# NSA's compressed branch in a slot table: minimum, exponential, normalising, transposes and evictions in slots of their own, probabilities transposed six slots behind

## The chip, the core and the metric

One core of a Trainium2 chip runs the whole program in one launch. The metric is the device time of that core in microseconds, the median of several runs. The engines are TensorE (PE, with its weight loads as PEld), VectorE (DVE), ScalarE (ACT), GpSimd (POOL) and SyncE (SP), which issues the DMAs. Each engine takes its instructions in the order in which the program wrote them, and the engines meet through semaphores.

## What is computed

One decoder layer over 512 tokens of width 1024: an input projection, three token mixers (NSA, a differential attention, a forgetting attention), gated merging, and a feed-forward part with a causal convolution. The change is in the compressed branch of the first mixer, NSA: each query looks at 31 compressed key blocks.

```python
def nsa_attention(q, k_cmp, v_cmp, k_slc, v_slc, k_win, v_win, gate_logits, cmp_end):
    ...
        dist_c = tpos[:, None] - cmp_end[None, :]
        s_c = jnp.einsum('btgrd,bngd->bgrtn', qg, k_cmp).astype(jnp.float32)
        s_c = s_c - sl[..., None] * dist_c.astype(jnp.float32)
        p_c = masked_softmax(s_c, dist_c >= 0)
        o_c = jnp.einsum('bgrtn,bngd->btgrd', p_c.astype(v_cmp.dtype), v_cmp)
        ...
        o = gc[:, :, 0] * o_c + gc[:, :, 1] * o_s + gc[:, :, 2] * o_w
```

With 512 tokens and eight selected blocks of 64 the selection takes every block, so the selected branch is plain causal attention (`slc`), beside a window of 256 (`win`).

## The kernel before, in words

Matrices are split into a high and a low part, and a product takes three matmuls (two where one factor is exact enough). While the attention of NSA runs, TensorE also works through the merge gates: 192 matmuls of 512 columns (G, "gate matmuls"), 40 of them before the attention's first unit, 152 spread over its slots. Weights for them arrive by DMA and are split by ScalarE (W, `wh`) and VectorE (WL, `wl`) in pieces of 512 columns.

`attention_events` (L121) writes the order of the stage as a table of slots, and every engine walks through the same list of events and does its own part of each. One slot is one *unit* j of 64: a query block i of 128 rows, one of eight heads, `slc` or `win`. A unit is

- S.j: TensorE two score matmuls over the unit's keys (128 to 512 columns) into bank 6 or 7; VectorE adds the bias and takes the minimum (`prob_n`, `nmx`, L1232); ScalarE takes the exponential and its sum (L867).
- C.j, for every second unit: VectorE forms the reciprocal and the coefficient (L1247, L1249), and GpSimd scales the two units' probabilities (L1470).
- Four units make a group, and each key block of a group is a step n: TA.n four transposes of `prob_n` on TensorE (L1559) into bank 4 or 5; EH.n ScalarE's high part `ptn_h` (L917); EL.n VectorE's low part `ptn_l` (L1267), which frees the bank for TA.n+2; VA.n two matmuls with the values (L1793, L1795) into bank 2 or 3, by the half g of the heads.
- When both groups of one g are through, OX.i.g copies half of the bank on ScalarE (`otmp_n`, L922), and VectorE sums it with the other half (`osum_n`, L1282, two instructions) and so frees the bank; OY.i splits the result for the projection.

The compressed branch adds for each query block i one job:

- SC.i: TensorE writes the scores of all eight heads with one matmul of 256 columns and sixteen of 32 columns (L1764 to L1768) into bank 2; VectorE takes minimum, difference and slope (L1303, L1304, L1307); ScalarE takes the exponential (L905).
- CN.i: VectorE sums, inverts, weighs by the gate and multiplies (L1312 to L1319).
- TC.i: TensorE transposes (L1774) into bank 2; ScalarE copies the high part `pcT` (L911); VectorE forms the low part (L1272).
- OC.i.g: TensorE multiplies with the compressed values (L1780), as the first product into bank 2 + g of block i.

Query block i begins at slot 16 i. SC.i stands in slot 16 i + 3, CN.i in + 5, TC.i in + 7. The first transposes of a group come `t_lag` = 5 slots behind its last unit, its first product three slots after them. Within a slot the tuple `order` (L220) sorts the events. For SC and TC all engines' parts stand in the same slot, since an event has one place in the list. The bank holds one result after the other in the order of the list: the sums of block i - 1, SC.i, TC.i, then block i; `begin` on TensorE waits until the result before has been taken.

## Time and profile before

| | us |
|---|---|
| median of three runs | 978.65 |
| the runs | 976.17, 978.65, 978.80 |
| the profiled execution | 978.79 |
| its span on the core | 977.0 |
| TensorE busy in it | 958.5 |
| VectorE busy | 559.8 |
| ScalarE busy | 426.2 |
| mean granted clock of TensorE | 0.996 |

The page says that TensorE is at work for nearly the whole span; "busy" counts a matmul from its start to a modelled end, so that rows overlap. The NSA stage lies at about 103 to 213 us: block 0 until 116, block 1 (units 16 to 31) until 138, block 2 until 168, block 3 until 200, then the last transposes and products without units. Everything before and behind it is projections, the other mixers and the feed-forward part.

### The profile page before, as it was taken

Reading aid. Unit: us, or ns where it says so; the run is one execution under the profiler, and the core shown is the slowest. Engines: PE = TensorE matmul, PEld = TensorE weight load, DVE = VectorE, ACT = ScalarE, POOL = GpSimd, SP = SyncE. Lnnn points to the kernel's source line nnn. Section 1 sums busy time; section 2 is a strip of 40 time slices with the busy share of each in tenths; the row PEclk is TensorE's granted clock in tenths of the full one; section 3 lists DMA queues with packets and bytes.
Section 4 is the critical chain, followed back from the end, with each engine's and each line's share of the span. In section 5 each row is a group of like instructions: output and inputs, shape, how many; then the busy total and the mean of one; then the engine's idle time right before and its main releaser. Section 6 shows DMA issues by size and latency. Waiting matters only on the chain.

```text
span 977.0 us, 12185 instructions
## 1 busy us (share of the span) xinstructions
PE 958.5 (98%) x4625; PEld 794.5 (81%) x4625; DVE 559.8 (57%) x1063; ACT 426.2 (44%) x770; POOL 209.8 (21%) x250
## 2 busy tenths in 40 slices
PE   6999999999999999999999999999999999999998
PEld 5787877788888888888888888888888888888887
DVE  6737787864366895546567454655655665522113
ACT  5335776754256653445777333423222322221110
POOL 3000457640001112212455220121112121100000
PEclk9999999999999999999999999999999999999999
DMA  6512110112222212222211242223222322232222
GB/s 237 219 44 86 45 44 1 43 45 86 87 89 85 87 44 87 86 87 87 81 50 44 87 172 87 87 89 123 91 87 87 121 95 86 87 117 99 87 87 86
DMA packets 13691, 86.33 MB, mean 88 GB/s; under 512 B 1473, under 2 KB 1985, under 8 KB 4289
## 3 DMA queue, kind: packets, MB, share of 16 engines
q1 hardware_dynamic: 13632, 85.55, 24.2%
q8 instruction: 37, 0.61, 0.3%
q14 instruction: 22, 0.17, 0.1%
HBM read 83.44 MB, written 2.10 MB: 88 GB/s over the span
## 4 chain that ended last, share of the span: by engine, by line
PE 89%; DVE 7%; ACT 2%; issue 2%; DMA 0%; SPq 0%; ACTq 0%; DVEq 0%
PE ps L1531 22%; PE ps L1533 22%; PE ps L1532 22%; PE ps L1715 10%; PE ps L1559 4%; PE ps L1672 1%; PE ps L1671 1%; PE ps L1700 1%; DVE prob_n L1232 1%; DVE wl L1013 1%; PE ps L1586 1%; DVE ptn_l L1267 1%; PE ps L1793 1%; PE ps L1795 1%; DVE prob L1232 1%
## 5 line engine op out<-in xcount | busy, mean ns | idle before, releaser
L1013 DVE TENSOR_TENSOR wl<-raw,wh 128x512 fp32r<-128x512 f32 (+2 forms) x118 | 173.5, 1475 | 136.4 <-ACT wh L701 133.8
L701 ACT ACTIVATE wh<-raw 128x2048 fp32r<-128x2048 f32 (+1 forms) x58 | 109.4, 1886 | 157.9 <-PE ps L1533 140.3
L1531 PE MATMUL ps<-aT_h,wh 128*128 128x512 f32 (+1 forms) x376 | 146.7, 390 | 0.8 <-DVE aT_l L1022 0.8
L1532 PE MATMUL ps<-aT_l,wh 128*128 128x512 f32 (+1 forms) x376 | 146.4, 389 | 0.0
L1533 PE MATMUL ps<-aT_h,wl 128*128 128x512 f32 (+1 forms) x376 | 146.4, 389 | 0.0
L1531 PE MATMUL ps<-wh,aT_h 128*128 128x512 f32 x256 | 102.0, 398 | 0.0
L1533 PE MATMUL ps<-wh,aT_l 128*128 128x512 f32 x256 | 100.0, 391 | 0.0
L1532 PE MATMUL ps<-wl,aT_h 128*128 128x512 f32 x256 | 99.8, 390 | 0.0
L1514 POOL TENSOR_TENSOR gl<-gl,rstdT 128x512 f32<-128x512 f32 x22 | 44.5, 2022 | 234.5 <-ACT gl L987 234.5
L1470 POOL TENSOR_SCALAR prob_n<-prob_n,coef 128x384 f32<-128x384 f32 (+3 forms) x64 | 67.7, 1071 | 114.6 <-DVE coef L1249 114.3
L1531 PEld LDWEIGHTS ps<-aT_h,wh 128*128 128x128 f32 (+1 forms) x376 | 70.0, 186 | 16.5 <-issue 1.0
L1533 PEld LDWEIGHTS ps<-aT_h,wl 128*128 128x128 f32 (+1 forms) x376 | 70.0, 186 | 15.3
L1532 PEld LDWEIGHTS ps<-aT_l,wh 128*128 128x128 f32 (+1 forms) x376 | 70.0, 186 | 15.0
L1715 PE MATMUL ps<-aT_h,wh 128*128 128x512 f32 x192 | 77.6, 404 | 0.1
L1715 PE MATMUL ps<-aT_l,wh 128*128 128x512 f32 x192 | 77.4, 403 | 0.0
L1715 PE MATMUL ps<-aT_h,wl 128*128 128x512 f32 x192 | 77.4, 403 | 0.0
L1531 PE MATMUL ps<-wh,actT_h 128*128 128x512 f32 x176 | 68.5, 389 | 0.0
L1532 PE MATMUL ps<-wl,actT_h 128*128 128x512 f32 x176 | 68.5, 389 | 0.0
L1533 PE MATMUL ps<-wh,actT_l 128*128 128x512 f32 x176 | 68.5, 389 | 0.0
L1533 PEld LDWEIGHTS ps<-wh,aT_l 128*128 128x128 f32 x256 | 48.0, 188 | 10.4
L1531 PEld LDWEIGHTS ps<-wh,aT_h 128*128 128x128 f32 x256 | 48.1, 188 | 9.5 <-issue 0.2
L1532 PEld LDWEIGHTS ps<-wl,aT_h 128*128 128x128 f32 x256 | 48.2, 188 | 9.4
(250 smaller groups left out, 1796.1 us busy)
## 6 DMA issues: line engine op xcount, KB each, us to landing
raw<-wblk SPq DMA_DIRECT2D x72, 1024.0 KB, 4.7
x<-x SPq DMA_DIRECT2D x4, 512.0 KB, 5.2
w_sb<-w SPq DMA_DIRECT2D x1, 2048.0 KB, 9.2
hid<-x SPq DMA_DIRECT2D x1, 2048.0 KB, 7.7
out<-outt SPq DMA_DIRECT2D x8, 256.0 KB, 2.0
stage<-consts SPq DMA_DIRECT2D x1, 708.5 KB, 4.7
later<-consts SPq DMA_DIRECT2D x1, 448.0 KB, 5.4
par<-params SPq DMA_DIRECT2D x1, 204.5 KB, 8.3
```

What stands on the lines that cost most here:

```text
L701: nc.scalar.activation(wh[b % 2][:, 0:n], raw[b % RING][:, 0:n], ACT.Copy).then_inc(hi_ready, 4)
L1013: ins = nc.vector.tensor_tensor(wl[b % RING][:, cols], raw[b % RING][:, cols], wh[b % 2][:, cols].bitcast(f32), ALU.subtract)
L1232: nc.vector.tensor_tensor_reduce(scores_at(m, j, n), ps[b][:, 0:n], bias, slope, 3e38, ALU.add, ALU.min, nmx[:, j:j + 1]).then_inc(psum_fr ...
L1267: nc.vector.tensor_tensor(ptn_l[j % PT_RING][:, :], ps[b][:, :], ptn_h[j % PT_RING][:, :].bitcast(f32), ALU.subtract).then_inc(psum_free[b ...
L1470: nc.gpsimd.tensor_scalar(p, p, coef[:, j:j + 1], None, ALU.mult).then_inc(pn_scaled, 1)
L1514: nc.gpsimd.tensor_tensor(gl[:, c, :], gl[:, c, :], rstdT[:, :], ALU.mult).then_inc(glr_ready, 1)
L1531: nc.tensor.matmul(dst, a_h, b_h, start=start, stop=False)
L1532: nc.tensor.matmul(dst, a_h, b_l, start=False, stop=False)
L1533: return nc.tensor.matmul(dst, a_l, b_h, start=False, stop=stop)
L1559: ins = nc.tensor.transpose(bk[:, n * P:(n + 1) * P], src, ident[:, :])
L1586: ins = nc.tensor.matmul(bk[:, 0:64], w1_sb[:, kv, r, :], cpe[:, kv, r], start=r == 0, stop=r == 15)
L1715: ins = nc.tensor.matmul(bk[:, :], (l if p == 2 else h)[:, k, cols], (aT_l if p == 1 else aT_h)[:, k], start=f % GATE_STEPS == 0, stop=f % ...
```

## The change

The list has new names, so that the engines' parts of one job get slots of their own. SC.i now is TensorE's scores alone, in slot 16 i + 3 as before; SCV.i is VectorE's minimum, difference and slope in + 4; SCA.i is ScalarE's exponential in + 5; CN.i is in + 6 (before + 5); TC.i, TensorE's transposes alone, in + 8 (before + 7); TCH.i, ScalarE's copy, and TCL.i, VectorE's low part, in + 9. `order` puts SCA and TCH first in their slots and SCV and TCL behind the units. `t_lag` and `o_lag` of NSA go from 5 and 10 to 6 and 11: every TA, EH, EL, VA, OX, OY and OC comes one slot later against the units and against SC, and the stage has 75 slots instead of 74. For i = 0 the order is as before.

```diff
-    t_lag, o_lag = {NSA: (5, 10), DIFF: (3, 5), FOX: (3, 5)}[m]
+    t_lag, o_lag = {NSA: (6, 11), DIFF: (3, 5), FOX: (3, 5)}[m]
...
             put(per * i + 3, "SC", i)
-            put(per * i + 5, "CN", i)
-            put(per * i + 7, "TC", i)
+            put(per * i + 4, "SCV", i)
+            put(per * i + 5, "SCA", i)
+            put(per * i + 6, "CN", i)
+            put(per * i + 8, "TC", i)
+            put(per * i + 9, "TCH", i)
+            put(per * i + 9, "TCL", i)
...
-    order = {k: n for n, k in enumerate(("GT", "EH", "OX", "OY", "OH", "OS", "FH", "S", "C", "OHL", "OSL", "FL", "EL", "OXL", "OYL","CN", "TC", "OC", "G", "SC", "FB", "VH", "VA", "TA", "A", "E", "O", "SUQ", "SUB", "SUG", "SUN", "OT", "WL", "W"))}
+    order = {k: n for n, k in enumerate(("SCA", "TCH", "GT", "EH", "OX", "OY", "OH", "OS", "FH", "S", "C", "OHL", "OSL", "FL", "EL", "OXL", "OYL","CN", "SCV", "TCL", "TC", "OC", "G", "SC", "FB", "VH", "VA", "TA", "A", "E", "O", "SUQ", "SUB", "SUG", "SUN", "OT", "WL", "W"))}
...
-                    elif what == "SC":
+                    elif what == "SCA":
                         act.wait_ge(pc_scaled, j + 1)
...
-                    elif what == "TC":
+                    elif what == "TCH":
...
-                    elif what == "TC":
+                    elif what == "TCL":
                         dve.wait_ge(pct_hi, j + 1)
...
-                    elif what == "SC":
+                    elif what == "SCV":
                         full(dve, ("SC", j))
```

The place of the job of block 1 on VectorE. Before, from the scores' minimum to the normalising (ISA with `prob_n` is a unit's bias and minimum):

```order
L1303 TENSOR_REDUCE cmx<-ps 128x8
L1304 TENSOR_TENSOR pc<-ps,cmx 128x256
L1307 TENSOR_TENSOR pc<-pc,slope_c 128x256
L1232 ISA prob_n_94,nmx<-ps,distW 128x256
L1232 ISA nmx 128x1
L1247 RECIPROCAL rl<-lsum 128x2
L1249 TENSOR_TENSOR coef<-rl,gsm 128x2
L1232 ISA prob_n_95,nmx<-ps,distW 128x256
L1232 ISA nmx 128x1
L1267 TENSOR_TENSOR ptn_l_87<-ps,ptn_h_84 128x512
L1312 TENSOR_REDUCE csum<-pc 128x8
```

The same stretch after the change (all line numbers are five higher from here on):

```order
L1308 TENSOR_REDUCE cmx<-ps 128x8
L1309 TENSOR_TENSOR pc<-ps,cmx 128x256
L1312 TENSOR_TENSOR pc<-pc,slope_c 128x256
L1237 ISA prob_n_95,nmx<-ps,distW 128x256
L1237 ISA nmx 128x1
L1237 ISA prob_n_96,nmx<-ps,distW 128x256
L1237 ISA nmx 128x1
L1252 RECIPROCAL rl<-lsum 128x2
L1254 TENSOR_TENSOR coef<-rl,gsm 128x2
L1272 TENSOR_TENSOR ptn_l_87<-ps,ptn_h_84 128x512
L1317 TENSOR_REDUCE csum<-pc 128x8
```

The minimum now stands behind the unit in `prob_n_94` and its coefficients (they are no longer between the two steps), and the unit in `prob_n_96` with its coefficients stands ahead of the sum.

The place ahead of SC.2 on VectorE, from a weight piece to the sum osum_n that frees bank 2. Before:

```order
L1013 TENSOR_TENSOR wl_54<-raw_51,wh_58 128x512
L1232 ISA prob_n_91,nmx<-ps,distD 128x384
L1232 ISA nmx 128x1
L1267 TENSOR_TENSOR ptn_l_89<-ps,ptn_h_86 128x512
L1282 TENSOR_TENSOR osum_n<-ps,otmp_n 64x256 x2
```

After:

```order
L1018 TENSOR_TENSOR wl_54<-raw_51,wh_58 128x512
L1237 ISA prob_n_91,nmx<-ps,distD 128x384
L1237 ISA nmx 128x1
L1237 ISA prob_n_92,nmx<-ps,distD 128x384
L1237 ISA nmx 128x1
L1252 RECIPROCAL rl<-lsum 128x2
L1254 TENSOR_TENSOR coef<-rl,gsm 128x2
L1272 TENSOR_TENSOR ptn_l_89<-ps,ptn_h_86 128x512
L1287 TENSOR_TENSOR osum_n<-ps,otmp_n 64x256 x2
```

One more unit and one pair of coefficients now stand ahead of the sum, while SC.2 has kept its slot.

The place ahead of SC.3 on TensorE. Before, the last transposes in the row ahead of it:

```order
L1715 MATMUL ps<-aT_l,wh_57 128x512
L1715 MATMUL ps<-aT_h,wl_56 128x512
L1559 MATMUL ps<-ident,prob_n_98 128x128
L1559 MATMUL ps<-ident,prob_n_99 128x128
L1559 MATMUL ps<-ident,prob_n_100 128x128
L1559 MATMUL ps<-ident,prob_n_101 128x128
L1671 MATMUL ps<-k_hh,q_hl 128x512
L1672 MATMUL ps<-k_ll,q_hl 128x512
L1715 MATMUL ps<-aT_h,wh_58 128x512
L1715 MATMUL ps<-aT_l,wh_58 128x512
L1764 MATMUL ps<-biasC,identr 128x256
```

After, from the last products of the bank's earlier result:

```order
L1798 MATMUL ps<-ptn_h_86,vn_hl 128x512
L1800 MATMUL ps<-ptn_l_89,vn_hl 128x512
L1564 MATMUL ps<-ident,prob_n_98 128x128
L1564 MATMUL ps<-ident,prob_n_99 128x128
L1564 MATMUL ps<-ident,prob_n_100 128x128
L1564 MATMUL ps<-ident,prob_n_101 128x128
L1676 MATMUL ps<-k_hh,q_hl 128x512
L1677 MATMUL ps<-k_ll,q_hl 128x512
L1785 MATMUL ps<-pcT,vc_hl 128x512
L1720 MATMUL ps<-aT_h,wl_56 128x512
L1720 MATMUL ps<-aT_h,wh_58 128x512
L1769 MATMUL ps<-biasC,identr 128x256
```

The products are now the last ones one slot before SC.3; before, they lie ahead of the first row shown, two slots before it.

## Rows read from the trace of the kernel before

**Rows 1.** The page: busy time, share of the span, instructions.

```profile
PE 958.5 (98%) x4625; PEld 794.5 (81%) x4625; DVE 559.8 (57%) x1063; ACT 426.2 (44%) x770; POOL 209.8 (21%) x250
```

**Rows 2.** Windows: stretch, length, busy us (instructions) per engine, clock, DMA, GB/s.

```profile
119.00:127.00 8.00, 6.52 (x45) 5.72 (x43) 5.86 (x24) 3.73 (x12) 3.66 (x4) 1.00 0.01 2
147.00:152.00 5.00, 5.00 (x22) 4.30 (x21) 2.56 (x10) 2.21 (x7) 3.35 (x3) 0.66 0.00 0
177.00:182.00 5.00, 5.00 (x21) 4.25 (x20) 4.09 (x12) 3.24 (x9) 3.08 (x2) 0.66 0.00 0
...
210.00:260.00 50.00, 50.00 (x223) 41.36 (x222) 23.11 (x26) 21.81 (x25) 3.61 (x2) 1.00 0.28 101
```

**Rows 3.** Timeline of TensorE, block 1: start, us, instruction, [idle before <-releaser].

```profile
121.83 0.26 PE L1767 MATMUL ps<-kc_hh,q_hl 128*128 128x32 f32 x1
121.94 0.26 PE L1768 MATMUL ps<-kc_l,q_hl 128*128 128x32 f32 x1
...
127.06 0.63 PE L1774 MATMUL ps<-ident,pc 128*64 128x128 f32 x4 [1.54 <-DVE pc L1319]
```

**Rows 4.** Timelines of VectorE and ScalarE, block 1.

```profile
122.24 0.42 DVE L1303 TENSOR_REDUCE cmx<-ps 128x8 f32<-128x256 f32 x1 [1.42 <-PE ps L1768]
...
123.50 0.42 DVE L1232 CUSTOM_DVE_ANT_0 prob_n<-ps,distW 128x256 f32<-128x256 f32 x1
...
123.84 0.16 DVE L1247 RECIPROCAL rl<-lsum 128x2 f32<-128x2 f32 x1
...
125.69 0.41 DVE L1312 TENSOR_REDUCE csum<-pc 128x8 f32<-128x256 f32 x1
...
126.58 0.43 DVE L1319 TENSOR_TENSOR pc<-pc,ccoef 128x256 f32<-128x256 f32 x1
...
129.16 0.69 DVE L1272 TENSOR_TENSOR pcT<-ps,pcT 64x512 fp32r<-64x512 f32 x1 [1.15 <-ACT pcT L911]
...
123.96 0.51 ACT L867 ACTIVATE prob_n<-prob_n,nmx 128x256 f32<-128x256 f32 x1
```

**Rows 5.** Timelines around the scores SC.2 and SC.3 and the sum before SC.2.

```profile
144.51 0.39 PE L1764 MATMUL ps<-biasC,identr 128*128 128x256 f32 x1 [0.29 <-DVE osum_n L1282]
...
174.62 0.39 PE L1764 MATMUL ps<-biasC,identr 128*128 128x256 f32 x1 [0.36 <-DVE osum_n L1282]
...
142.98 0.59 ACT L922 ACTIVATE otmp_n<-ps 64x512 f32<-64x512 f32 x1
...
143.61 0.85 DVE L1282 TENSOR_TENSOR osum_n<-ps,otmp_n 64x256 f32<-64x256 f32 x2
```

**Rows 6.** Timeline of TensorE: the waits of blocks 2 and 3.

```profile
153.50 0.63 PE L1774 MATMUL ps<-ident,pc 128*64 128x128 f32 x4 [0.42 <-DVE pc L1319]
...
159.82 0.65 PE L1559 MATMUL ps<-ident,prob_n 128*128 128x128 f32 x4 [0.64 <-DVE ptn_l L1267]
...
189.48 0.50 PE L1671 MATMUL ps<-k_hh,q_hl 128*128 128x512 f32 x1 [0.39 <-DVE nmx L1232]
...
191.54 0.66 PE L1559 MATMUL ps<-ident,prob_n 128*128 128x128 f32 x4 [0.61 <-DVE ptn_l L1267]
```

**Rows 7.** Timeline of VectorE: the low part of pcT, blocks 2 and 3.

```profile
156.53 0.69 DVE L1272 TENSOR_TENSOR pcT<-ps,pcT 64x512 fp32r<-64x512 f32 x1 [1.26 <-ACT pcT L911]
...
187.41 0.68 DVE L1272 TENSOR_TENSOR pcT<-ps,pcT 64x512 fp32r<-64x512 f32 x1 [0.66 <-ACT pcT L911]
```

**Rows 8.** Timelines of GpSimd and VectorE where both read SBUF.

```profile
145.42 2.47 POOL L1470 TENSOR_SCALAR prob_n<-prob_n,coef 128x384 f32<-128x384 f32 x2 [1.12 <-DVE coef L1249]
...
147.54 0.42 DVE L1307 TENSOR_TENSOR pc<-pc,slope_c 128x256 f32<-128x256 f32 x1
...
178.92 3.11 POOL L1470 TENSOR_SCALAR prob_n<-prob_n,coef 128x512 f32<-128x512 f32 x2 [2.51 <-DVE coef L1249]
...
179.08 1.07 DVE L1013 TENSOR_TENSOR wl<-raw,wh 128x512 fp32r<-128x512 f32 x1 [0.26 <-ACT wh L704]
...
183.02 0.68 DVE L1013 TENSOR_TENSOR wl<-raw,wh 128x512 fp32r<-128x512 f32 x1
```

More of the change, by code:

```diff
@@ L224, in attention_events @@
         b = BI[(m, "gate1")]
-        first = [("G", 0, 8), ("SC", 0), ("W", b, 0), ("G", 8, 16), ("CN", 0), ("WL", b, 0), ("W", b, 1), ("G", 16, 24), ("GT", 0), ("T", 0), ("WL", b, 1),
-                 ("W", b, 2), ("G", 24, 28), ("TC", 0), ("G", 28, 32), ("T", 1), ("WL", b, 2), ("W", b, 3), ("WL", b, 3), ("G", 32, head)]
+        first = [("G", 0, 8), ("SC", 0), ("SCV", 0), ("SCA", 0), ("W", b, 0), ("G", 8, 16), ("CN", 0), ("WL", b, 0), ("W", b, 1), ("G", 16, 24), ("GT", 0), ("T", 0), ("WL", b, 1),
+                 ("W", b, 2), ("G", 24, 28), ("TC", 0), ("TCH", 0), ("TCL", 0), ("G", 28, 32), ("T", 1), ("WL", b, 2), ("W", b, 3), ("WL", b, 3), ("G", 32, head)]
     if m == FOX:
```

## The prediction, as it was written before the change was run

> **What bounds the kernel now.** I read the page's busy line first: TensorE is busy 958.5 of 977.0 us [rows 1], so the time can only change where TensorE waits or where its clock is halved. After the stage that the change touches, from 210 to 260 us, it is busy 50.00 of 50.00 us [rows 2]: a microsecond lost or won in the stage goes straight to the end. Then the TensorE timeline of the stage, 103 to 213 us, where the waits are single rows with an idle time in brackets, and the VectorE timeline beside it for what VectorE was doing when TensorE waited. The losses come in three rounds, one for each compressed job i = 1, 2, 3.
>
> Round 1: the last compressed-score matmul starts at 121.94, and the transposes TC.1 start at 127.06 after 1.54 us of idling for VectorE's normalising [rows 3]. Round 2: the scores SC.2 wait 0.29 us for the bank that the sum osum_n frees [rows 5], TC.2 waits 0.42, and then the transposes of probabilities at 159.82 wait 0.64 for VectorE's low part [rows 6]. Round 3: SC.3 waits 0.36 [rows 5], a unit's scores at 189.48 wait 0.39 and transposes at 191.54 wait 0.61 [rows 6]. A wait costs TensorE some 0.15 us more than the idle time in its row, since modelled ends overlap: matmuls listed as 0.26 us long start 0.11 us apart [rows 3]. On top, the granted clock is 0.66 in 147 to 152 us and in 177 to 182 us, against 1.00 around round 1 [rows 2]: (1 - 0.66) x 5 = 1.7 us each.
>
> VectorE and ScalarE work strictly in the written order, and VectorE's own idle rows show what the order costs: it stands 1.42 us before the minimum of SC.1 [rows 4], and before the low part of pcT 1.15 us in round 1 [rows 4], 1.26 in round 2 and 0.66 in round 3 [rows 7], since that step asks ScalarE for a copy of transposes which TensorE has only just issued. The change aims at these.
>
> **The change part by part.** No instruction is added or removed and no DMA moves in its queue; every cost is one of order. The number of slots goes from 74 to 75 and the 152 gate matmuls are spread over them, so mostly one gate matmul less has been issued at a given slot; they are issued later, at the same price.
>
> *Round 1, minimum and normalising.* From the last score matmul to TC.1 there were 127.06 - 121.94 = 5.1 us. In the new order VectorE has between them: the bias-and-minimum of the next unit (0.43: the 0.42 us row of rows 4), its coefficients (two operations of 0.16 with a gap, some 0.35), minimum, subtraction and slope (three times 0.42), the next unit (0.43), a further unit (0.43) with coefficients (0.35) that wait for that unit's exponential on ScalarE (0.51 and a read behind it, [rows 4]), one low part (0.7, as the 0.69 row of rows 4) and the normalising, 125.69 to 127.01, so 1.3 [rows 4]. With 0.4 us until the first unit's scores are there, and about 0.4 of waiting for exponential and high part, that is 0.4 + 0.43 + 0.35 + 1.26 + 0.43 + 0.43 + 0.35 + 0.4 + 0.7 + 1.3 = 6.05 us. TensorE can put only one more unit and two gate matmuls before TC.1 (about 0.7 us). So the wait of 1.54 us does not go: it becomes 1.54 + (6.05 - 5.1) - 0.7 = about 1.8 us. I take **+0.3 us** for the round, since the first product with pcT then also waits for VectorE's low part, which now stands behind the osum_n sums; the ends are -0.6 (the waits for exponential and high part vanish, and the 1.15 us of [rows 4] is turned into work) and +0.8.
>
> *Rounds 2 and 3, the bank of the compressed scores.* SC.i needs the bank whose earlier contents osum_n adds up. With the transposes six slots behind, this sum moves from slot 33 to 34 before SC.2 (slot 35) and from 50 to 51 before SC.3, which stays in slot 51. SC.2: before, VectorE went from the low part to the sum with one unit fewer in front; ScalarE's copy for it started at 142.98 and the sums ran 143.61 to 144.45, and SC.2 started at 144.51, at once [rows 5]. VectorE was without a pause, so the unit that now comes in front (384 columns against the 256 of the 0.42 us row, say 0.55) and its two coefficient operations (0.35), which wait for an exponential just begun (0.3), push the sums back by 1.2 us. TensorE has nothing else in its order but one gate matmul less. **+1.2 us**, ends +0.4 (the waits for the weight pieces in the slots before give something back) and +1.8. SC.3: before, two slots of TensorE work lay between the last product into that bank and SC.3, now one. A slot there is a unit (2 x 0.23), two gate matmuls and mostly transposes and two products, some 1.7 us; the way from product over ScalarE's copy and VectorE's sum gets shorter by about 0.5, since less stands in front of it. **+1.2 us**, ends +0.5 and +1.8.
>
> *What the spreading gives back.* After SC.2, TC.2 comes a slot later, and TensorE gets one more unit and a gate matmul or two to fill its 0.42 us; VectorE's 1.26 us before the pcT step goes, since the transposes are now a slot older than the copy and the low part. This takes the 0.64 behind it as well. 0.42 + 0.64 and twice 0.15, with 0.14 for shorter waits further on: **-1.5 us**, ends -0.6 and -1.8. After SC.3 the same: 0.39 + 0.61 + 0.3 = 1.3 could go, but the weight pieces WL stand in the same slots and one low part is still late; **-0.9 us**, ends -0.3 and -1.3.
>
> *The lag of six for its own sake.* The transposes of probabilities wait in the trace for VectorE's low parts, which move with them, and in no row for GpSimd, which scales the probabilities. So a slot more there hides nothing: 0, ends -0.3 and +0.3. The eleven slots at the end have no units, and TensorE runs through them without a wait now.
>
> *The clock.* Both falls follow a run of seventeen narrow matmuls that stood behind a short wait. The waits before them grow, so I keep both falls at 1.7 us each: 0, ends -1.7 (one goes) and +1.7 (a third).
>
> *A rule that speaks against the moved step.* The slope multiplication reads two SBUF operands. It now comes right after a unit's coefficients, and these start GpSimd on two scalings: 2.47 us for two at 384 columns, 1.24 us each, and 3.11 for two at 512 [rows 8]. The trace has one such meeting: the slope multiplication at 147.54 started under the GpSimd pair of 145.42 to 147.89 and took 0.42 us, like all the others [rows 4, 8]. Against it stands the weight piece at 179.08, under the pair from 178.92: 1.07 us, where the one at 183.02 took 0.68 [rows 8]. So something is there, of 0 to 0.4 us. I take 0 for the sum, the row of the same instruction. The Trainium skill (SBUF — State Buffer, section "SBUF: two separate sides") says that VectorE with two SBUF inputs and a GpSimd operation take turns on one pair of ports, and that the one which comes second is blocked until the first is done. By that rule the three slope steps would cost some 0.3 to 0.6 us each, and the sum would be about 1 us higher; the meeting at 147.54 disagrees with it.
>
> **The sum**, against the profiled execution: +0.3 + 1.2 - 1.5 + 1.2 - 0.9 = +0.3 us. That execution took 978.79 us, 1.79 more than its span, and lies 0.14 above the median of the runs, 978.65. Forecast: **979.1 us**. A measurement of this kernel can tell about 0.3%, 2.9 us, from no change; the three runs alone lie 2.6 us apart. What the spreading gives in each round, the later sum takes.
>
> **The rivals.**
>
> *Faster, 975.5 us.* VectorE is what the stage waits for, and its idle rows (1.15 + 1.26 + 0.66 = 3.1 us) turn into work in full, while the sums still come in time for SC.2 and SC.3 because VectorE runs ahead. Then round 1 gives 1.5, rounds 2 and 3 give 1.8 and 1.3, and the later sum costs 0.6 twice: 978.8 - 4.6 + 1.2 = 975.4, say 975.5. For it: all waits of rows 6 name VectorE. Against: at SC.2 and SC.3 the sum was already the last to come, and it is moved the wrong way. 0.17.
>
> *Slower, 982 us.* The longer waits before the narrow matmuls bring the clock down once more, behind SC.1 with its wait of 1.8 us for TC.1, or keep it down longer at SC.2. The price is 1.7 us by rows 2, and the waits before SC.2 and SC.3 are then at their upper ends, 0.6 us more each: 979.1 + 1.7 + 1.2 = 982.0. It decides once the wait before TC.1 or before SC.2 is clearly longer than the 1.54 us that passed at full clock. For it: both falls came behind a wait of only 0.29 and 0.36 us and the narrow run. Against: around TC.1 1.54 us of waiting went by at full clock [rows 2]. 0.20.
>
> *The turn-taking at the ports, 980.1 us.* GpSimd's scalings hold up the three slope steps: 1.24 - 0.9 = 0.3 us at 384 columns and 1.55 - 0.9 = 0.6 at 512, as the slope comes some 0.9 us behind the coefficients, in all about 1 us. The rule of the Trainium skill (SBUF — State Buffer) gives this. 0.05; it stays within 0.3%.
>
> **How the numbers follow.** The forecast has 0.58. Its own ends, not all at once, are about 976.8 and 981.4. Faster by over 0.3% (under 975.7) has the faster rival's 0.17, slower by over 0.3% (over 981.6) most of the slower one's 0.20 and 0.01 from the rest, the same has 0.58 + 0.05 less that 0.01, so 0.62. For 8 in 10 the range takes in half of each rival's weight: 975.3 to 982.3.
>
> **What would show it.** Right: TensorE's row of SC.2 and of SC.3 carries over 1 us of idling for osum_n; TC.1 still waits 1.3 to 2 us; TC.2 and the two or three transposes behind it wait for nothing; VectorE's idling before the pcT rows is under 0.4 us in all rounds; two stretches at about 0.66 clock. Wrong: waits before SC.2 and SC.3 of under 0.6 us (then the faster rival), a third stretch of low clock (the slower one), slope rows longer than 0.42 us (the ports), or a wait for GpSimd anywhere in the stage.

## The result, and the profile after

| | before | changed |
|---|---|---|
| median of 20 runs each, us | 978.24 | 980.25 |
| range, us | 975.51 to 979.00 | 977.76 to 980.96 |
| ratio, 95% interval | | 1.0023 [1.0015, 1.0030] |
| profiled execution / its span, us | 978.79 / 977.0 | 980.96 / 979.2 |
| mean granted clock of that execution | 0.996 | 0.994 |

The changed kernel is 2.0 us slower: inside the 0.3% taken as no change, on its slower side, and with an interval that doesn't reach 1. The times of one kernel fall into groups some 2.5 us apart, and a median depends on how many runs are in each. Every run lists its mean granted clock, and the groups go with it, though not strictly. The 73 runs of the kernel before that were made beside the experiments take 975.29 to 976.51 us at 1.00 and 978.49 to 979.74 at 0.996 or 0.997, but at 0.998 eight take 975.96 to 976.55 and twelve 977.92 to 978.54.

The page and the windows of the changed kernel; the columns are those of [rows 1, 2]. Line numbers are 5 higher than before.

```profile
PE 958.9 (98%) x4625; PEld 795.1 (81%) x4625; DVE 560.2 (57%) x1063; ACT 425.8 (43%) x770; POOL 211.1 (22%) x250
...
142.00:147.00 5.00, 3.60 (x20) 3.11 (x20) 3.22 (x10) 3.51 (x9) 3.48 (x4) 0.83 0.01 3
147.00:152.00 5.00, 5.00 (x15) 4.38 (x16) 2.55 (x9) 1.51 (x4) 2.40 (x2) 0.50 0.00 0
...
177.00:182.00 5.00, 5.00 (x28) 4.56 (x28) 2.53 (x9) 1.82 (x4) 1.70 (x2) 0.74 0.35 146
182.00:187.00 5.00, 4.97 (x28) 3.89 (x27) 4.10 (x14) 3.84 (x9) 3.64 (x3) 0.92 0.00 0
...
210.00:260.00 50.00, 50.00 (x226) 41.41 (x225) 23.06 (x27) 20.51 (x26) 3.61 (x2) 1.00 0.25 86
```

Busy times are those of before, and TensorE is again busy without a gap behind the stage. What differs, beside the waits below, is the clock: (0.17 + 0.50 + 0.26 + 0.08) x 5 = 5.05 us lost against 3.4 before [rows 2]. In 147 to 152 us TensorE ran at 0.50 throughout, its lower level of 1.2 GHz. So the clock takes three times 1.7 us here, twice at SC.2, where it took two before. That the third lengthens a run can't be seen in the times: eleven other runs of the changed kernel have mean clocks of 0.996 or 0.997 and take 980.23 to 980.95 us, as this one at 0.994 does.

TensorE's four waits of over 1 us in the stage, from its timeline; the idle time is in the brackets.

```profile
127.19 0.63 PE L1779 MATMUL ps<-ident,pc 128*64 128x128 f32 x4 [1.79 <-DVE pc L1324]
...
144.57 0.39 PE L1769 MATMUL ps<-biasC,identr 128*128 128x256 f32 x1 [1.41 <-DVE osum_n L1287]
...
156.61 0.62 PE L1779 MATMUL ps<-ident,pc 128*64 128x128 f32 x4 [1.04 <-DVE pc L1324]
...
176.40 0.39 PE L1769 MATMUL ps<-biasC,identr 128*128 128x256 f32 x1 [1.45 <-DVE osum_n L1287]
```

Against [rows 3, 5, 6]: TC.1 1.54 became 1.79, SC.2 0.29 became 1.41, TC.2 0.42 became 1.04, SC.3 0.36 became 1.45; the waits of 0.64 and 0.39 are gone, the one of 0.61 stayed, with 0.58.

The low clock begins inside the narrow matmuls that follow the wait for SC.2. TensorE's timeline there:

```profile
144.94 0.26 PE L1772 MATMUL ps<-kc_hh,q_hl 128*128 128x32 f32 x1
145.05 0.26 PE L1773 MATMUL ps<-kc_l,q_hl 128*128 128x32 f32 x1
...
145.72 0.37 PE L1773 MATMUL ps<-kc_l,q_hl 128*128 128x32 f32 x1
145.94 0.37 PE L1772 MATMUL ps<-kc_hh,q_hl 128*128 128x32 f32 x1
```

They start 0.11 us apart before 145.3 and 0.21 apart from 145.5 on. In the kernel before, all seventeen of SC.2 ran at full clock, and the fall came at 147 us.

**Where the 2.2 us between the two spans lie.** The first 95 us hold nothing of the change but the head's entries, and they vary from one execution to the next. The normalising of block 0, in VectorE's timelines of before and of after:

```profile
96.08 0.43 DVE L1319 TENSOR_TENSOR pc<-pc,ccoef 128x256 f32<-128x256 f32 x1
```

```profile
95.29 0.43 DVE L1324 TENSOR_TENSOR pc<-pc,ccoef 128x256 f32<-128x256 f32 x1
```

It starts anywhere from 94.65 to 96.58 in the fourteen profiles taken for this study, kernels with and without the change alike. The span behind that row is therefore the cleaner measure: 977.0 - 96.08 = 880.9 us before, 979.2 - 95.29 = 883.9 after, **+3.0**. By the rows, 5.05 - 3.4 = 1.6 us of this are clock and 1.7 us are waits (TensorE's listed waits in 103 to 213 us sum to 6.6 us after and 4.9 before), 3.3 in all. The 0.8 us that the head ran earlier in this execution bring the +3.0 down to +2.2.

This division isn't firm. The same row in the second profiles of the two kernels (experiments 11 and 12, spans 974.5 and 975.8), before and then after:

```profile
95.47 0.42 DVE L1319 TENSOR_TENSOR pc<-pc,ccoef 128x256 f32<-128x256 f32 x1
```

```profile
95.02 0.42 DVE L1324 TENSOR_TENSOR pc<-pc,ccoef 128x256 f32<-128x256 f32 x1
```

They leave 879.0 us before and 880.8 after, +1.8, with 1.7 us of low clock on the changed side alone and 1.0 us more of listed waits (6.5 against 5.5): 2.7 by the rows, 1.8 in time. Without its low clock the changed kernel would take about 879.1 us there, as long as the kernel before. That is an estimate, since no run of the changed kernel was at full clock; by these two pairs, what its waits alone cost lies between about nothing and 1.7 us.

### The profile page after: what moved, and what is told of

It is laid out like the page before. It is cut to its first block, busy times and chain, and to the rows that moved or that the text cites. A ratio compares the mean times of both kernels' runs of the same rounds, so it can differ in the third digit from the quotient of the medians.

```text
span 979.2 us, 12185 instructions
## 1 busy us (share of the span) xinstructions
PE 958.9 (98%) x4625; PEld 795.1 (81%) x4625; DVE 560.2 (57%) x1063; ACT 425.8 (43%) x770; POOL 211.1 (22%) x250
## 4 chain that ended last, share of the span: by engine, by line
PE 89%; DVE 6%; ACT 2%; issue 2%; DMA 1%; SPq 0%; DVEq 0%; ACTq 0%
PE ps L1536 22%; PE ps L1538 22%; PE ps L1537 22%; PE ps L1720 10%; PE ps L1564 4%; PE ps L1677 1%; PE ps L1676 1%; PE ps L1705 1%; DVE wl L1018 1%; DMA par<-params 1%; DVE prob_n L1237 1%; PE ps L1591 1%; PE ps L1798 1%; PE ps L1800 1%; DVE ptn_l L1272 1%
```

## The experiments

The theories: **A**, the one slot more of lag does the harm: it moves osum_n up against SC.2 and SC.3, and this wait, with the clock that falls behind it, is the price. **B**, the finer slots do it: VectorE's steps now stand behind other work, and the loss would stay at the old lag. **C** (later): it takes the unbroken run of narrow matmuls behind the wait to bring the clock down. **D** (later): the clock falls when TensorE waits over 1 us just ahead of the narrow matmuls. The median stands first in each result, with the ratio to runs of the kernel before on the same chip and its 95% interval. The experiments ran on three chips, on which the kernel before has medians of 978.04 (1 to 4), 976.38 (5 to 8) and 978.54 (9 and 10), so that kernels of different groups are compared by their ratios. "Runs at full clock" are those whose mean granted clock is listed as 1.00.

### 1. The new slots at the old lag

```diff
-    t_lag, o_lag = {NSA: (6, 11), DIFF: (3, 5), FOX: (3, 5)}[m]
+    t_lag, o_lag = {NSA: (5, 10), DIFF: (3, 5), FOX: (3, 5)}[m]
```

> The change without its lag: minimum, exponential, normalising, transposes and evictions in slots of their own, but transposes of probabilities five slots behind as before. Theory A (the later osum_n sum does the harm, the slots of their own give something back): the waits for osum_n before SC.2 and SC.3 are back at 0.3 to 0.5 us instead of 1.41 and 1.45, and the kernel is 1.5 to 3 us faster than before, 975.5 to 977. Theory B (the slots of their own do the harm, since more stands before the normalising): TC.1 and TC.2 wait as long as with the whole change (1.8 and 1.0 us) and the kernel is 1 to 2.5 us slower than before.

980.83 us, 1.0034 [1.0020, 1.0048]; 4 of 10 runs at full clock, at 978.99 to 979.86. TensorE's timeline of one of these (span 977.5):

```profile
133.23 0.47 PE L1785 MATMUL ps<-pcT,vc_hl 128*128 128x512 f32 x1 [2.40 <-DVE pcT L1277]
...
145.00 0.39 PE L1769 MATMUL ps<-biasC,identr 128*128 128x256 f32 x1 [0.25 <-DVE osum_n L1287]
...
191.49 0.48 PE L1785 MATMUL ps<-pcT,vc_hl 128*128 128x512 f32 x1 [1.96 <-DVE pcT L1277]
```

A was half right, and the 975.5 to 977 us that it gave did not come. The wait of SC.2 went back to 0.25, and SC.3's to 0.35, so the lag is what lengthens them. But the compressed product L1785, which is placed by the lag, now comes one slot behind the new slot of pcT's low part and waits 2.40, 1.44 and 1.96 us for it. B's loss is there, at a place that B did not name. So the two halves of the change need each other: the low part could be moved back only because the lag moved the product away.

### 2. The lag alone, on the kernel before

```diff
-    t_lag, o_lag = {NSA: (5, 10), DIFF: (3, 5), FOX: (3, 5)}[m]
+    t_lag, o_lag = {NSA: (6, 11), DIFF: (3, 5), FOX: (3, 5)}[m]
```

> The lag without the slots: transposes of probabilities six slots behind, the compressed jobs written as before. Theory A: over 1 us of waiting for osum_n before SC.2 and SC.3, the longer stretch of low clock stays, and what the slots gave back is missing: 3 to 5 us slower than before. Theory B: the lag costs nothing, the kernel is within 1 us of before.

981.69 us, 1.0043 [1.0026, 1.0059]. The profile happens to be of its one run at full clock, 976.60; the waits are there:

```profile
144.18 0.38 PE L1764 MATMUL ps<-biasC,identr 128*128 128x256 f32 x1 [1.42 <-DVE osum_n L1282]
...
171.97 0.39 PE L1764 MATMUL ps<-biasC,identr 128*128 128x256 f32 x1 [1.45 <-DVE osum_n L1282]
```

The other six runs have mean clocks of 0.992 to 0.996 and take 980.13 to 981.95. So the lag alone makes both waits and costs 3.6 us, and at full clock its one run is only 0.3 to 1.1 us above the ten runs of before at full clock beside it (975.55 to 976.25). By this one run, most of the loss is in the clock.

### 3. The changed kernel with its compressed job one slot later

```diff
-            put(per * i + 3, "SC", i)
-            put(per * i + 4, "SCV", i)
+            put(per * i + 4, "SC", i)
+            put(per * i + 5, "SCV", i)
...
-            put(per * i + 9, "TCH", i)
-            put(per * i + 9, "TCL", i)
+            put(per * i + 10, "TCH", i)
+            put(per * i + 10, "TCL", i)
```

> The whole change, and the compressed jobs of blocks 1 to 3 one slot later still, so that the sum osum_n stands as far ahead of SC as before the change. Theory A: waits of 0.3 to 0.5 us before SC.2 and SC.3, the clock falls as briefly as before the change, 1.5 to 3 us faster than before. Theory B: as with the whole change, 1 to 2.5 us slower than before, since the normalising has the same work ahead of it.

980.16 us, 1.0025 [1.0014, 1.0036]; 4 of 12 runs at full clock, at 978.44 to 978.95. SC.2 and SC.3 wait only 0.40 and 0.21 now, and the products are hit as in experiment 1:

```profile
134.59 0.47 PE L1785 MATMUL ps<-pcT,vc_hl 128*128 128x512 f32 x1 [2.40 <-DVE pcT L1277]
```

With the job cut into these slots, there is one slot too few for it between the sum that frees the bank and the first product with pcT, at each of the three places tried.

The clock of this profile falls twice, and the first fall has no narrow matmuls just ahead of it:

```profile
132.00:137.00 5.00, 2.60 (x11) 2.04 (x10) 4.07 (x14) 3.84 (x11) 2.40 (x3) 0.88 0.19 29
137.00:142.00 5.00, 5.00 (x26) 4.24 (x26) 2.89 (x10) 3.52 (x9) 2.50 (x4) 0.78 0.44 182
```

It costs (0.12 + 0.22) x 5 = 1.7 us and comes behind the wait of 2.40 us for pcT, under matmuls of 256 and 512 columns. Experiment 1 waits as long at the same place at full clock.

### 4. A bank of their own for the compressed scores

The scores of blocks 1 to 3 go to the two banks of the transposes (4 and 5, in turn) instead of bank 2, so they no longer wait for osum_n; no slot changes.

```diff
+            elif e[0] == "SC" and e[1]:
+                plan_t(("SC", e[1]))
             elif e[0] in ("SC", "TC"):
                 plan((e[0], e[1]), 2 if e[1] else spare)
```

> The whole change, but the compressed scores of blocks 1 to 3 go to the banks that the transposes use in turn, so that they don't wait for the sum osum_n. Theory A: no wait for osum_n ahead of SC; perhaps one for a low part ptn_l of 0 to 0.7 us in its place; 1 to 3 us faster than before. Theory B: 1 to 2.5 us slower than before.

974.82 us, 0.9983 [0.9972, 0.9995], that is 5.4 us under the changed kernel's median (by the two ratios to before, 0.9983 and 1.0023, it is 3.9 us). A had given 1 to 3 us less than before, and by the medians it is 3.2. Seven of 12 runs are at full clock, against none of the changed kernel's 20, and take 974.05 to 974.85; the other five, at 0.998, take 976.45 to 976.88. Waits and clock of a run at full clock:

```profile
143.23 0.39 PE L1771 MATMUL ps<-biasC,identr 128*128 128x256 f32 x1 [0.65 <-DVE ptn_l L1274]
...
147.00:152.00 5.00, 4.04 (x24) 3.22 (x22) 4.18 (x14) 2.90 (x9) 4.26 (x4) 1.00 0.01 2
```

SC.2 now waits 0.65 for a transpose bank, SC.3 for nothing. TC.1 waits 1.75 us, as in the changed kernel, and passes at full clock.

### 5. The narrow matmuls broken up

Two of the gate matmuls of the slot (which are 512 columns wide) are put among the narrow ones, behind the sixth and the twelfth of them.

```diff
-                        for f in range(e[1], e[2]):
+                        inside = list(range(e[1], e[2])) if late[0] == "SC" and late[1] else []
+                        for f in range(e[1], e[2]) if not inside else ():
...
                             ins = nc.tensor.matmul(dst, q_hl[:, h, rows], kc_l[:, h // 4, h % 2], start=False, stop=h == 7)
+                            if j and h in (2, 5) and inside:
+                                gate_step(inside.pop(0))
```

> The whole change, but the two gate matmuls of the slot stand among the narrow matmuls of SC.1 to SC.3 instead of ahead of them. They no longer cover the wait for the bank: by the waits alone this costs 2 x 0.46 = 0.9 us, 981.2. Theory C (the longer wait together with the unbroken run of seventeen narrow matmuls is what brings the clock down for 3.4 and 1.8 us in the profile of the change): the low-clock stretches shrink or go, and the time is 977 to 979.5. If the waits alone decide, the clock stays low as long as with the change, and the time is 981 to 982.

981.95 us, 1.0046 [1.0028, 1.0065], no run of 6 at full clock (0.993 to 0.997). The gate matmuls no longer stand in front of SC, so the wait grew, and the low clock at SC.2 lasted as long as in the changed kernel:

```profile
145.05 0.38 PE L1771 MATMUL ps<-biasC,identr 128*128 128x256 f32 x1 [1.88 <-DVE osum_n L1287]
...
147.00:152.00 5.00, 5.00 (x17) 4.52 (x18) 1.98 (x7) 0.82 (x3) 1.29 (x2) 0.50 0.00 0
```

C falls in the form in which it was put: an unbroken run is not needed. The edit changes two things at once, wait and run, so it doesn't tell which of them made it worse than the changed kernel.

### 6. Own bank, and the transposes of pc one slot later

```diff
-            put(per * i + 8, "TC", i)
-            put(per * i + 9, "TCH", i)
-            put(per * i + 9, "TCL", i)
+            put(per * i + 9, "TC", i)
+            put(per * i + 10, "TCH", i)
+            put(per * i + 10, "TCL", i)
...
-                put(end + t_lag + 2, "OC", i, g)
+                put(end + t_lag + (3 if i else 2), "OC", i, g)
```

> As the kernel whose compressed scores have their own bank, and TC, TCH, TCL and the first product of blocks 1 to 3 one slot later. If what is left there is TensorE coming to TC before VectorE has normalised (1.75 and 1.03 us of waiting), these waits shrink by a slot each, to about 0.8 and 0.1, and 1 to 1.7 us are won over that kernel: 973 to 974. If the wait comes back one slot later in the product (as in the kernel without the lag, 2.40, 1.44 and 1.96 us for pcT), it is as fast as that kernel or up to 3 us slower.

977.73 us, 1.0000 [0.9987, 1.0012], by the ratios 1.7 us above experiment 4; 4 of 12 at full clock, at 975.09 to 976.09 against 974.05 to 974.85 there. TC no longer waits, and what stood behind it does:

```profile
127.25 0.38 PE L1678 MATMUL ps<-k_hh,q_hl 128*128 128x256 f32 x1 [1.06 <-DVE nmx L1239]
...
132.72 0.47 PE L1787 MATMUL ps<-pcT,vc_hl 128*128 128x512 f32 x1 [1.54 <-DVE pcT L1279]
```

VectorE is what is late in block 1; giving TensorE's step more room passes the lateness on.

SC.2 waits 0.72 us here, and the clock of this profile falls as long as in the changed kernel, where it waits 1.41:

```profile
142.00:147.00 5.00, 4.28 (x24) 3.74 (x24) 3.21 (x9) 3.08 (x9) 3.04 (x3) 0.78 0.01 3
147.00:152.00 5.00, 5.00 (x17) 4.02 (x16) 2.28 (x9) 1.83 (x5) 2.47 (x2) 0.53 0.01 2
```

(0.22 + 0.47) x 5 = 3.45 us are lost. So the long fall does not need the long wait.

### 7. The kernel before, with the own bank alone

The edit of experiment 4 on the kernel before.

> The kernel before, with nothing changed but the bank of the compressed scores of blocks 1 to 3: the banks that the transposes use in turn. By its waits (0.29 and 0.36 us for osum_n, with 0.15 each) at most 1 us is to be had: 977.0 to 978. If the bank also decides over the clock, its faster group of runs becomes the usual one: 974.5 to 976.

974.74 us, 0.9976 [0.9966, 0.9986]; nine of 11 runs at full clock and two at 0.999, all between 974.21 and 975.48. In the 29 runs of the kernel before beside it, eleven were at full clock (975.29 to 976.30) and the rest reached up to 979.74. The clock is 1.00 in every window of the profiled run; the one of 147 to 152 us:

```profile
147.00:152.00 5.00, 4.56 (x29) 3.86 (x28) 4.33 (x17) 3.66 (x10) 3.35 (x3) 1.00 0.01 2
```

The shared bank cost the kernel before, too: 1.2 us at full clock (median of those runs 975.88 against 974.65) and, in most runs, a fall of the clock.

### 8. Normalising first in its slot

On VectorE the normalising CN is written ahead of the slot's minimum and coefficients of the unit, instead of behind them and a low part. In the order of kinds within a slot:

```diff
-    order = {k: n for n, k in enumerate(("SCA", "TCH", "GT", "EH", "OX", "OY", "OH", "OS", "FH", "S", "C", "OHL", "OSL", "FL", "EL", "OXL", "OYL","CN", "SCV", "TCL", "TC", "OC", "G", "SC", "FB", "VH", "VA", "TA", "A", "E", "O", "SUQ", "SUB", "SUG", "SUN", "OT", "WL", "W"))}
+    order = {k: n for n, k in enumerate(("SCA", "TCH", "GT", "EH", "OX", "OY", "OH", "OS", "FH", "CN", "S", "C", "OHL", "OSL", "FL", "EL", "OXL", "OYL", "SCV", "TCL", "TC", "OC", "G", "SC", "FB", "VH", "VA", "TA", "A", "E", "O", "SUQ", "SUB", "SUG", "SUN", "OT", "WL", "W"))}
```

> The whole change, but the normalising stands first in its slot on VectorE, ahead of the unit, its coefficients and the low part. If it is this work ahead of the normalising that keeps TC.1 and TC.2 waiting (1.79 and 1.04 us), these waits fall under 0.5 us; the units' minimum comes 1.3 us later in that slot and may cost 0.3 to 0.6 us of waiting for nmx. 978 to 979.5 by the waits. If the waits only move (to units, transposes or the product), 980 to 981 as with the change.

979.51 us, 1.0018 [1.0008, 1.0029]; one of 13 runs at full clock, 974.38, and this is the profiled one. VectorE's timeline of its normalising in block 1, and TensorE's row of SC.2. Between the slope step and the sum stands only one unit's minimum now, and the normalising is done at 124.9 instead of 127.1 us; 0.6 of these 2.2 us are the head, which ran earlier in this execution.

```profile
123.59 0.42 DVE L1317 TENSOR_REDUCE csum<-pc 128x8 f32<-128x256 f32 x1
...
124.48 0.43 DVE L1324 TENSOR_TENSOR pc<-pc,ccoef 128x256 f32<-128x256 f32 x1
...
143.55 0.39 PE L1769 MATMUL ps<-biasC,identr 128*128 128x256 f32 x1 [1.41 <-DVE osum_n L1287]
```

TC.1 and TC.2 wait for nothing, so it was the place in the slot that made them wait; 0.73 and 0.63 us came back at a unit's scores and at a product, and transposes of block 3 wait 1.30 us. SC.2 and SC.3 wait 1.41 and 1.45 as ever, and 12 of 13 runs have low clock. Against the changed kernel the ratio falls by 0.0005 only, well inside the intervals.

### 9. Both mends

Experiments 4 and 8 together, on the changed kernel.

> The whole change with both mends: compressed scores in the banks of the transposes, and the normalising first in its slot. By the waits: the kernel with the normalising first took 974.4 in its run without a fall of the clock, and loses there 1.41 and 1.45 us before SC.2 and SC.3, of which some 0.65 stays as a wait for a low part: 972 to 973.5. Theory D (the clock falls when TensorE waits over 1 us just ahead of the narrow matmuls): no falls in nearly all runs, so the median is that same time. If the clock falls whatever the wait is, a group of runs 2 to 5 us above it holds the median: 975 to 977.

**974.03 us, 0.9957 [0.9941, 0.9974]**, 972.44 to 974.75 in 6 runs, three of them at full clock: it beats both kernels. Against experiment 4 the ratio is 0.0026 lower, some 2.5 us, with intervals that overlap a little. D does not hold as it was put: no wait ahead of the narrow matmuls is over 1 us, which was to leave nearly all runs without a fall, and three of six have low clock. The profiled run (974.75) has one fall:

```profile
144.14 0.38 PE L1771 MATMUL ps<-biasC,identr 128*128 128x256 f32 x1 [0.64 <-DVE ptn_l L1274]
...
147.00:152.00 5.00, 5.00 (x21) 4.17 (x20) 3.90 (x16) 2.43 (x6) 2.46 (x2) 0.67 0.01 2
```

### 10. Nine narrow matmuls for seventeen

This kernel leaves out the products with the low part of the compressed keys in blocks 1 to 3 (the eight L1773), which is a part of the computation.

```diff
-                            nc.tensor.matmul(dst, q_hl[:, h, rows], kc_hh[:, h // 4], start=False, stop=False)
-                            ins = nc.tensor.matmul(dst, q_hl[:, h, rows], kc_l[:, h // 4, h % 2], start=False, stop=h == 7)
+                            ins = nc.tensor.matmul(dst, q_hl[:, h, rows], kc_hh[:, h // 4], start=False, stop=j > 0 and h == 7)
+                            if j == 0:
+                                ins = nc.tensor.matmul(dst, q_hl[:, h, rows], kc_l[:, h // 4, h % 2], start=False, stop=h == 7)
```

> The whole change, with the products of the low part of the compressed keys left out for blocks 1 to 3, so that nine narrow matmuls stand in SC.1 to SC.3 instead of seventeen. The waits of 1.41 and 1.45 us for the bank stay, the narrow run is halved. By the work alone 3 x 8 x 0.11 = 2.6 us are saved, of which 1 to 2.6 reach the end: 977.7 to 979.3. If it is the length of the narrow run that brings the clock down, the falls go as well and the time is 973 to 975. If the wait does it, 977.7 to 979.3 stays.

976.46 us, 0.9987 [0.9977, 0.9997], eleven of 12 runs at a mean clock of 0.998 and one at 0.996. The matmuls left out take 3 x 8 x 0.11 = 2.6 us at full clock; the median is 3.8 us under the changed kernel's (3.5 by the ratios), between the two results that were expected. The wait is unchanged. The fall behind SC.2 costs 1.7 us instead of 3.35, and there is none behind SC.3:

```profile
144.70 0.39 PE L1769 MATMUL ps<-biasC,identr 128*128 128x256 f32 x1 [1.40 <-DVE osum_n L1287]
...
147.00:152.00 5.00, 5.00 (x22) 4.17 (x21) 2.63 (x12) 2.64 (x7) 2.46 (x2) 0.66 0.01 2
```

One profile doesn't show more, since the changed kernel's second profile has a single fall too; but of the changed kernel's 20 runs only eight are at 0.998, of these 12 eleven. So the narrow matmuls have a part in how much low clock there is, and the wait alone does not explain it.

### 11 and 12. Both kernels profiled once more

> The kernel before, once more, for a second profile. Its runs come in two groups, near 975.6 and near 978.6. If the groups differ by the clock alone, a profile of the lower group has the same waits as the first profile (0.29 and 0.36 us before SC.2 and SC.3, 1.54 before TC.1) and no stretch under 1.00.

> The changed kernel, once more, for a second profile. Its runs come in two groups, near 978.0 and 980.5, and the first profile is of the upper one. Theory D: the same waits again, with at least one stretch of low clock behind SC.2 or SC.3; in a run of the lower group one stretch is missing or shorter, by about 2.5 us of time.

Before: 976.24 us, full clock in every window. The waits ahead of the first fall are as in the first profile (TC.1 1.51, SC.2 0.29), and so is SC.3 with 0.35. Behind it they are longer in block 3: a unit's scores wait 0.90 instead of 0.39, and TC.3 waits 0.22 instead of nothing.

```profile
186.84 0.50 PE L1671 MATMUL ps<-k_hh,q_hl 128*128 128x512 f32 x1 [0.90 <-DVE nmx L1232]
```

After: 977.55 us, the waits as in the first profile (1.76, 1.41, 1.02, 1.45, 0.58), and full clock around SC.2. The window of before, then the two of after:

```profile
147.00:152.00 5.00, 4.58 (x28) 3.81 (x27) 4.05 (x17) 3.06 (x8) 2.78 (x3) 1.00 0.00 0
```

```profile
172.00:177.00 5.00, 4.05 (x26) 3.86 (x27) 1.53 (x6) 1.66 (x5) 1.19 (x1) 0.83 0.58 210
177.00:182.00 5.00, 5.00 (x26) 4.37 (x25) 4.54 (x14) 4.05 (x11) 3.79 (x3) 0.83 0.00 0
```

With the same waits up to the fall, one execution of a kernel has it and another has not. The whole times differ by 2.55 us for the kernel before (3.4 us of low clock against none) and by 3.41 for the changed one (5.05 against 1.7). Behind the normalising of block 0 it is 880.9 - 879.0 = 1.9 us and 883.9 - 880.8 = 3.1. So the lost clock is paid nearly in full in the changed kernel, and only in part in the kernel before, where while TensorE is slow VectorE catches up and waits of block 3 shrink by 0.7 us.

### All kernels side by side

| kernel | wait of SC.2 / SC.3 in its profile, us | runs at full clock | times of those, us | median, us |
|---|---|---|---|---|
| before (beside the experiments) | 0.29 / 0.36 | 27 of 73 | 975.29 to 976.51 | 976.38 to 978.54 |
| changed | 1.41 / 1.45 | 0 of 20 | none | 980.25 |
| 1 old lag | 0.25 / 0.35 | 4 of 10 | 978.99 to 979.86 | 980.83 |
| 2 lag alone | 1.42 / 1.45 | 1 of 7 | 976.60 | 981.69 |
| 3 job later | 0.40 / 0.21 | 4 of 12 | 978.44 to 978.95 | 980.16 |
| 4 own bank | 0.65 / none | 7 of 12 | 974.05 to 974.85 | 974.82 |
| 5 broken up | 1.88 / 1.91 | 0 of 6 | none | 981.95 |
| 6 own bank, TC later | 0.72 / none | 4 of 12 | 975.09 to 976.09 | 977.73 |
| 7 before, own bank | none / none | 9 of 11 | 974.21 to 975.48 | 974.74 |
| 8 CN first | 1.41 / 1.45 | 1 of 13 | 974.38 | 979.51 |
| 9 own bank, CN first | 0.64 / none | 3 of 6 | 972.44 to 973.80 | 974.03 |
| 10 nine narrow | 1.40 / 1.45 | 0 of 12 | none | 976.46 |

Kernels whose scores wait 1.4 us or more have 2 of 58 runs at full clock; those that wait at most 0.72 us have 58 of 136. The two runs of the 58 and the second profile of the changed kernel show that such a wait does not have to bring the clock down; the first profile of the kernel before and those of experiments 6 and 9 show falls behind waits of 0.29, 0.72 and 0.64 us. The counts also hold whatever else differs between the kernels, and in experiment 3 a fall came at another place.

## Why the prediction was right, and where it was not

The forecast was 979.1 us with "the same" as the likeliest. The profiled execution took 980.96 and the median is 980.25: in the range, and 1.2 us above the forecast. By its steps:

- **Round 1, +0.3.** Right. TC.1 was to wait about 1.8 us and waits 1.79 (1.54 before). VectorE's pause before the pcT rows, 1.15 us before [rows 4], went, as was said.
- **SC.2 and SC.3, +1.2 each.** Right, and the core of it. They wait 1.41 and 1.45 for osum_n, 1.1 us more than before at each; experiments 1 and 2 show that the lag makes these waits, 4 and 7 that the shared bank carries them.
- **TC.2 and what is behind it, -1.5.** This step failed. It said that one unit and a gate matmul more on TensorE would fill the 0.42 us, and that VectorE's 1.26 us of idling would be turned into use. The idling went (before the four pcT rows together VectorE now idles 0.2 us), but TC.2 waits 1.04. The normalising stands in its slot behind a unit's minimum, coefficients and low part, and in block 2 VectorE has to wait for this unit's scores:

```profile
153.54 0.56 DVE L1237 CUSTOM_DVE_ANT_0 prob_n<-ps,distW 128x384 f32<-128x384 f32 x1 [1.97 <-PE ps L1677]
...
154.30 0.69 DVE L1272 TENSOR_TENSOR ptn_l<-ps,ptn_h 128x512 fp32r<-128x512 f32 x1
...
155.78 0.77 DVE L1324 TENSOR_TENSOR pc<-pc,ccoef 128x256 f32<-128x256 f32 x1
```

  VectorE idled 1.97 us for the scores L1677, while the exponential had been ready since 151.2. It then did 0.69 us of another unit's low part, and only then the sum. The half clock up to 152 us made this idling longer, but it does not make the wait: in the second profile, at full clock here, VectorE idles only 0.64 us and TC.2 waits just as long. VectorE's and TensorE's rows there:

```profile
150.12 0.56 DVE L1237 CUSTOM_DVE_ANT_0 prob_n<-ps,distW 128x384 f32<-128x384 f32 x1 [0.64 <-PE ps L1677]
...
153.18 0.62 PE L1779 MATMUL ps<-ident,pc 128*64 128x128 f32 x4 [1.02 <-DVE pc L1324]
```

  The prediction weighed this order in round 1 and left it out in round 2. Experiment 8 shows that with the normalising first the wait is gone. Of the 1.5 us, the 0.64 at 159.82 did go, with the 0.15 that it carries; TC.2 took 0.62 back. The step was worth about -0.2.
- **Round 3 behind SC.3, -0.9.** Roughly right: 0.39 went and 0.61 stayed, 0.58 now. About -0.6, and more against the kernel before at full clock, where the wait that went is 0.90.
- **The clock, 0.** Mis-sized. It was to keep two falls at 1.7 us each and its end was +1.7 for a third. There are still two stretches, but the first is twice as long, 3.35 us by the windows: +1.6 in the profiled execution. This is a part of the rival "slower", whose other wording was "keep it down longer at SC.2"; its place was right, and its point of decision, a wait before SC.2 clearly longer than 1.54 us, was not: it came with 1.41 us in this execution and with 0.72 in experiment 6, and did not come with 1.41 in the changed kernel's second profile. The reasoning compared with TC.1, where 1.54 us (and 1.79 now) pass at full clock; what follows there are transposes and not seventeen narrow matmuls, and experiment 10 shows that these matter.
- **The sum.** By these terms +0.3 + 1.1 + 1.1 - 0.2 - 0.6 = +1.7 us of waits, which is also what the listed waits give, and +1.6 of clock, together 3.3 where +3.0 was measured. The 0.8 us of the head, which no step could foresee, brought the profiled execution down to +2.2. So the forecast of +0.3 was 1.3 us short in the TC.2 step, 0.3 in round 3 and 1.6 in the clock. That it came out 1.2 us from the median is in part luck: the head, the low clock that was not paid in full, and the groups of runs took back what these steps missed. That it kept the slower rival at 0.20 and reached to 982.3 was what the clock called for.
- **The lag for its own sake, 0.** As far as can be seen right: no wait in the stage names GpSimd.
- **The faster rival.** VectorE's idling before pcT did turn into work and the time fell only where the sum didn't come late: with bank and order mended (experiment 9) the median is 4.5 us under that of before, somewhat more than the 3.1 us which the rival gave, and some of it is clock. Its mechanism was sound as far as VectorE's idling goes, and the sums stood in its way, as the text said against it.
- **The ports.** The slope steps did come under GpSimd's scalings and were not held up:

```profile
122.56 1.95 POOL L1475 TENSOR_SCALAR prob_n<-prob_n,coef 128x256 f32<-128x256 f32 x2 [1.02 <-DVE coef L1254]
...
123.29 0.43 DVE L1312 TENSOR_TENSOR pc<-pc,slope_c 128x256 f32<-128x256 f32 x1
```

  All four slope rows take 0.42 to 0.43 us. The prediction set a rule against this (the Trainium skill, SBUF — State Buffer, section "SBUF: two separate sides"): of VectorE and GpSimd, the one that comes second is blocked until the first is done. By it the step at 123.29 would wait for the end of a scaling that began at 122.56 and takes 0.98; the rows disagree with it. The next section has a case in which something of the kind does appear.

**What stays open.** Why the clock falls in one execution and not in another with the same waits; the runs show only how often it does. What the longer waits cost at full clock, for want of such a run of the changed kernel. Where the low clock of the eight runs of the kernel before lies that are at 0.998 and no slower than those at 1.00. How much of a fall is due to the wait and how much to the narrow matmuls behind it was not told apart: experiment 5 changed both, experiment 10 only the matmuls. The other runs of experiments 2 and 8 (most of them 5 us above their one run at full clock) list mostly mean clocks of 0.992 to 0.995, but no profile of them was taken, so where in them the clock was low is inferred from the other kernels.

## What to carry to other kernels

When a lag is changed, look up every consumer whose place is not given by it: here the scores SC kept their slot while the sum that frees their bank moved towards them. Before re-timing such a pair, see whether the result can go to another bank; this one line was worth more than every shift of slots tried here, and with the old slots it gave 2.3 us (ratio 0.9976). And in a profile with two levels of clock, compare runs of equal clock first and count how many reach it: the two say different things, what the waits cost and what they set off.

## What the runs showed of the hardware that was not expected

- **The same program falls or does not.** Two profiles of one kernel, with waits equal to 0.03 us up to the fall, differ by 2.55 and 3.41 us; of this 1.9 and 3.1 us lie behind the head, against 3.4 us of lost clock in both pairs. The mean clock of the runs (0.992 to 1.00) goes with groups of times some 2 to 5 us apart, with the exception at 0.998 told in the first section.
- **Shorter waits of TensorE were worth more than their length in the median, and less at equal clock.** From the changed kernel to experiment 4 the waits before the scores shrank by 1.41 + 1.45 - 0.65 = 2.2 us and the median by 5.4 (by the ratios, the time by 3.9). Behind the head, the changed kernel's second profile less its 1.7 us of low clock is 879.1 us and experiment 4's, at full clock, 877.6: some 1.5 us, an estimate. The rest is clock.
- **A VectorE operation with two SBUF inputs is held up if it starts right behind the start of a GpSimd scaling.** The normalising product of 155.78 took 0.77 us where its like takes 0.43. The scalings of that moment are

```profile
154.48 2.47 POOL L1475 TENSOR_SCALAR prob_n<-prob_n,coef 128x384 f32<-128x384 f32 x2 [2.41 <-DVE coef L1254]
```

  two of 1.24 us, so the second began at about 155.72, 0.06 us ahead. The same is seen at 186.16 (0.78 us, a scaling from about 186.09), in experiment 4 at 151.23 (0.78, from about 151.17) and before at 179.08 (1.07 instead of 0.68, from 178.92 [rows 8]). In these rows the delay is 0.34 to 0.39 us, not the rest of the scaling. Where the distance is 0.21 us, in experiment 2, the normalising product takes 0.52:

```profile
123.16 1.83 POOL L1470 TENSOR_SCALAR prob_n<-prob_n,coef 128x256 f32<-128x256 f32 x2 [1.95 <-DVE coef L1249]
...
124.29 0.52 DVE L1319 TENSOR_TENSOR pc<-pc,ccoef 128x256 f32<-128x256 f32 x1
```

  Steps that start 0.6 us or more behind the start of a scaling, and under it, take their usual 0.42 or 0.43 (179.59 in experiment 4, the slope steps above). It made up a third of the wait of TC.2; no run was made for it alone.
